# Residual and read-back products at the end of an expert pass placed elsewhere in TensorE's order, one tile's second result added by VectorE

## The reference

```python
combine = jnp.sum(jax.nn.one_hot(e_idx, N_EXPERTS, dtype=F32) * weights[..., None], axis=1)
a = jnp.einsum('td,edf->tef', x, w_gate)
b = jnp.einsum('td,edf->tef', x, w_up)
hid = jax.nn.silu(a) * b * combine[:, :, None].astype(x.dtype)
y = jnp.einsum('tef,efd->td', hid, w_down)
...
x = x + g2 * hierarchical_moe(h, ...)
```

## Time and profile before

| what | value |
|---|---|
| runs | 787.0, 788.08, 793.8 us, median 788.08 |
| span of the profiled execution | 789.8 us, its only recorded time |
| TensorE busy | 663.3 us, 84% |
| VectorE busy | 295.1 us, 37% |
| ScalarE, GpSimd busy | 132.0 us, 121.6 us |
| DMA over the span | 369 GB/s on average, 291.11 MB |
| share of the chain that ended last | PE 64%, DMA 27%, DVE 4% |

### The profile page before, as it was taken

The page is one execution under the profiler, slowest core; times in us unless marked ns, Lnnn a source line. Parts: engine busy times, 40 slices in busy tenths (PEclk is TensorE's granted clock), DMA queues, the critical chain, the costliest instruction groups (busy, mean ns, idle before and its releaser), DMA issues.

```text
span 789.8 us, 12765 instructions
## 1 busy us (share of the span) xinstructions
PE 663.3 (84%) x4709; PEld 361.2 (46%) x4709; DVE 295.1 (37%) x723; ACT 132.0 (17%) x328; POOL 121.6 (15%) x194
## 2 busy tenths in 40 slices
PE   3899999999998999999546668998999997564576
PEld 3443443446886855554213223648655553221232
DVE  2305518664217434444211131555444443112123
ACT  3111134553045100000000000653000000000000
POOL 1000000001000223333221010010234334111010
PEclk9999999999998899999866788998999999677679
DMA  9999859868189389999999999997599999999995
GB/s 334 426 429 428 335 224 395 353 284 356 56 357 395 121 354 418 420 418 417 421 423 421 423 420 350 426 424 316 184 420 416 419 420 421 423 421 419 421 403 232
DMA packets 39577, 291.11 MB, mean 369 GB/s; under 512 B 7466, under 2 KB 8898, under 8 KB 20448
## 3 DMA queue, kind: packets, MB, share of 16 engines
q1 hardware_dynamic: 30112, 272.46, 83.5%
q0 software_dynamic: 7600, 12.81, 4.7%
q10 hardware_dynamic: 1808, 5.06, 1.6%
HBM read 284.68 MB, written 17.56 MB: 383 GB/s over the span
## 4 chain that ended last, share of the span: by engine, by line
PE 64%; DMA 27%; DVE 4%; SPq 2%; issue 1%; ACT 1%; DVEq 0%; ACTq 0%
PE bank L1725 17%; DMA adaw<-in_moe_w_in 9%; PE bank L1430 8%; DMA ring<-in_moe_w_in 8%; PE bank L1762 7%; DMA adas<-in_moe_w_in 7%; PE bank L1355 4%; PE bank L1529 4%; DMA ring<-in_ada_w 3%; PE bank L1684 2%; PE bank L1537 2%; PE bank L1468 2%; PE bank L1489 2%; PE bank L1644 2%; PE bank L1592 1%; PE bank L1500 1%
## 5 line engine op out<-in xcount | busy, mean ns | idle before, releaser
L1725 PE MATMUL bank<-ring,qkv 128*32 128x256 f32 (+1 forms) x1344 | 140.7, 447 | 46.6 <-DMA ring<-in_moe_w_in 33.6
L1725 PEld LDWEIGHTS bank<-ring,qkv 128*32 128x32 f32 (+1 forms) x1344 | 78.2, 139 | 93.4 <-issue 66.8
L1201 DVE COPY qkv<-bank 128x512 f32<-128x512 f32 x44 | 30.5, 692 | 205.9 <-PE bank L1684 205.9
L603 POOL DMA_INDIRECT results<-adaw,scur x46 | 47.3, 1029 | 265.0 <-DVE adaw L1224 226.3
L868 ACT ACTIVATE qkv<-bank 128x128 f32<-128x128 f32 x48 | 13.3, 278 | 419.2 <-PE bank L1725 419.2
L1762 PE MATMUL bank<-ring,qkv 128*32 128x512 f32 (+1 forms) x368 | 65.7, 601 | 0.0
L1430 PE MATMUL bank<-ring,hT 128*128 128x512 f32 x144 | 63.8, 597 | 1.3 <-DVE hT L948 1.3
L1725 PE MATMUL bank<-seventh,qkv 128*64 128x256 f32 (+1 forms) x224 | 34.8, 478 | 16.4 <-DMA ring<-in_moe_w_in 16.4
L593 POOL DMA_INDIRECT adaw<-rows,gcur x40 | 41.7, 1042 | 33.0 <-POOL gcur L590 27.7
L1725 PE MATMUL bank<-adaw,qkv 128*64 128x256 f32 (+1 forms) x256 | 35.8, 442 | 10.0 <-DMA adas<-in_moe_w_in 10.0
L1430 PEld LDWEIGHTS bank<-ring,hT 128*128 128x128 f32 x144 | 26.7, 190 | 37.0 <-issue 35.8
(11 more groups left out here) (265 smaller groups left out, 856.2 us busy)
## 6 DMA issues: line engine op xcount, KB each, us to landing
ring<-in_moe_w_in SPq DMA_DIRECT2D x37, 2048.0 KB, 20.7
ring<-in_moe_w_out SPq DMA_DIRECT2D x44, 1024.0 KB, 24.1
ring<-in_ada_w SPq DMA_DIRECT2D x14, 2048.0 KB, 14.8
adaw<-in_ada_w SPq DMA_DIRECT2D x10, 2048.0 KB, 16.0
adaw<-in_moe_w_in SPq DMA_DIRECT2D x8, 2048.0 KB, 23.6
seventh<-in_moe_w_in SPq DMA_DIRECT2D x8, 1792.0 KB, 26.2
xT<-in_moe_w_in SPq DMA_DIRECT2D x8, 1536.0 KB, 19.1
hT<-in_moe_w_out SPq DMA_DIRECT2D x10, 1024.0 KB, 26.2
```

The lines of the kernel that those rows point to most:

```text
L603: pool.indirect_dma_start(res, bass.IndirectOffsetOnAxis(ap=scur[:, p, :], axis=0), yout[:, p], None, bounds_check=res_limit, oob_is_err=F ...
L1201: V.tensor_copy(xgT[:, p], bank[2][:, :]).then_inc(xgT_ready, 1)
L1725: last = T.matmul(bank[p][64 * a + m * h:64 * a + m * (h + 1), 0:2 * P], xk[:, k % 4, k // 4, m * h:m * (h + 1)], gate_up_of(b, k)[:, :, a ...
```

## The change

It moves three things and replaces one.

1. On TensorE `residual` of the first tile stands ahead of the second-last `step`, that of the third tile behind it (with a wait for the last row transpose's copy), that of the second tile behind `down(NS - 2)` and a wait for VectorE's result of tile NS - 2. All three are ahead of the last `gate_up`.
2. The first tile's second-result product stands ahead of the one-hot products, the second tile's behind them.
3. The third tile (token tile 0) has no second-result product; VectorE adds that result to xtok with one 128x1024 add, after it has added the first. `sum_mm` counts in another order, and VectorE adds the first results in the order tile 1, tile 0, tile 2.
4. The read-backs come in the order second, first for the first two tiles, first, second for the third.

```diff
                 sp.wait_ge(results_in, l + 1)
-                for t in TILES_BACK:
-                    for k in range(2):
+                for n, t in enumerate(TILES_BACK):
+                    for k in ((1, 0), (1, 0), (0, 1))[n]:
...
+            def first_result(l, t, n):
                 dve.wait_ge(s_xin[t][0], l * 16 + 16)
-                dve.wait_ge(sum_mm, l * TT + n + 1)
+                dve.wait_ge(sum_mm, l * TT + n)
...
+            def summed(l, n):
+                t = TILES_BACK[n]
+                if n == 0:
+                    first_result(l, t, 1).then_inc(x_sum, 1)
+                    order(first_result(l, TILES_BACK[2], 2))
+                elif n == 1:
+                    first_result(l, t, 3).then_inc(x_sum, 1)
+                else:
+                    dve.wait_ge(s_xin[t][1], l * 16 + 16)
+                    V.tensor_tensor(xtok[:, t, :], xtok[:, t, :], parts[t][:, 1, :], ALU.add).then_inc(x_sum, 1)
...
-                for s in range(1, NS - 1):
+                for s in range(1, NS - 2):
                     step(s)
...
                 residual(TILES_BACK[0])
+                step(NS - 2)
+                pe.wait_ge(xgT_ready, l * NS + NS)
+                residual(TILES_BACK[2])
                 down(NS - 2, (NS - 2) % 2)
+                pe.wait_ge(y_ready, l * NS + NS - 1)
+                residual(TILES_BACK[1])
                 gate_up(NS - 1, (NS - 1) % 2)
                 hidden_T(NS - 1, (NS - 1) % 2)
-                pe.wait_ge(y_ready, l * NS + NS - 1)
-                residual(TILES_BACK[1])
-                residual(TILES_BACK[2])
                 down(NS - 1, (NS - 1) % 2)
...
+                second_result(TILES_BACK[0], False)
+                pe.wait_ge(y_ready, l * NS + NS)
+                last_tile(TILES_BACK[0], True).then_inc(sum_mm, 1)
+                last_tile(TILES_BACK[1], False)
+                last_tile(TILES_BACK[2], True).then_inc(sum_mm, 1)
+                second_result(TILES_BACK[1], True).then_inc(sum_mm, 1)
```

More of the change, by code:

```diff
@@ L1297, in scale_tile @@
                 V.tensor_scalar(part, part, ss[:, 12 + t:13 + t], None, ALU.mult).then_inc(band_ready, 1)
-            def summed(l, n):
-                t = TILES_BACK[n]
+            def first_result(l, t, n):
                 dve.wait_ge(s_xin[t][0], l * 16 + 16)
-                dve.wait_ge(sum_mm, l * TT + n + 1)
+                dve.wait_ge(sum_mm, l * TT + n)
                 for a, b in enumerate(SUM_BANKS[t]):
@@ L1307, in summed @@
                         order(last)
-                last.then_inc(x_sum, 1)
+                return last
+            def summed(l, n):
[8 more added lines that the diff above has]
+                    V.tensor_tensor(xtok[:, t, :], xtok[:, t, :], parts[t][:, 1, :], ALU.add).then_inc(x_sum, 1)
             scales(1, 1, 8)
@@ L1815, in _, with second_result, last_tile @@
                     residual(TILES_BACK[2])
-                pe.wait_ge(y_ready, l * NS + NS)
-                for t in TILES_BACK:
+                def second_result(t, stop):
+                    pe.wait_ge(s_xin[t][1], l * 16 + 16)
+                    for a, b in enumerate(SUM_BANKS[t]):
+                        last = T.matmul(bank[b][:, :], ident, parts[t][:, 1, a * 512:(a + 1) * 512], start=False, stop=stop,
+                                        skip_group_check=True)
+                    return last
+                def last_tile(t, stop):
                     for a, b in enumerate(SUM_BANKS[t]):
                         half = slice(64 * a, 64 * a + 64)
[L1820 to L1825, removed]
-                                        skip_group_check=True)
-                    last.then_inc(sum_mm, 1)
+                        last = T.matmul(bank[b][:, :], dg[half, t], yout[half, (NS - 1) % NBUF], start=False, stop=stop,
+                                        skip_group_check=True)
+                    return last
+                second_result(TILES_BACK[0], False)
[4 more added lines that the diff above has]
+                second_result(TILES_BACK[1], True).then_inc(sum_mm, 1)
                 if l == 0:
```

## The result

| | kernel before | changed kernel |
|---|---|---|
| runs and median | 20 runs, 790.64 us | 20 runs, 787.03 us |
| ratio to before | | 0.9943, 95% interval 0.9923 to 0.9963 |
| profiled span | 789.8 us | 785.6 us |

By the ratio the change gains 0.57%, 4.5 us (2.9 to 6.1). The three runs that stood ahead of the prediction had a median of 788.08; with twenty the kernel before is at 790.64. The medians are 3.6 us apart, which lies inside the same interval. A fp32 product stands in all these traces as two records, so four records are the two products of a tile.

What follows compares the result with a forecast made beforehand. The prediction took TensorE's chain of products, behind each pass's last gate product, to bound the pass ends. Gains of 4.3 and 4.7 us minus 2.2 for the clock gave 6.8: 788.08 - 6.8 = 781.3 us, range 778.0 to 786.0.

Steps and rivals of the forecast that it cites:

- the price of the clock: TensorE's new pauses in both passes may drop the clock to 1.2 GHz: 0 to 4.5 us, taken as 2.2.
- step 1: Two residual tiles leave TensorE's path ahead of the last down product, which starts 3.0 us sooner in pass 1.
- Step 2 and 3: Closing read-back products and VectorE's reordered sums in pass 1: last sum ends at 496.7 us, before at 499.91.
- Step 4: From pass 1's last sum to the next stage's windows 2.23 us: windows at 498.95 instead of 503.23, 4.3 us gained.
- The second pass: Pass 2 moves with pass 1's gain; at its end the last add comes at 782.05 instead of 786.77, 4.7 us.
- rival B: Both new TensorE pauses cost their full clock price: 788.08 - 4.5 = 783.6 us; chance 0.22 together with E.
- Rival A: The clock costs nothing in either pass: 788.08 - 9.0 = 779.1 us; chance 0.22.
- Rival C: Read-backs land later, so VectorE's hold is 2 us longer in each pass, on top of the clock: 785.3; chance 0.10.
- D: Fifth read-back lands so late, 6 us in each pass, that the kernel gets slower: 791 us; chance 0.04.
- E: New wait for VectorE's result delays the last gate product, so residuals stay on the path: about 784; 0.22 with B.

Runs made afterwards that it cites:

- the two agreeing profiles: Second and third profile of the unchanged kernel before; the three stretches sum to 307.4 us in each, against 310.7 in its first profile.
- the sums alone: Changed kernel with the residual products where they were before; only the new read-back order, second-result products and VectorE sums remain; ratio 0.9961 (0.9926 to 0.9997), 3.1 us.
- the second set: Second timing of the kernel before with only the residual products moved: 12 runs, ratio 1.0004 (0.9975 to 1.0033); the first timing gave 1.0028 in 10 runs.

## Why the prediction was right or wrong

The forecast was 781.3 with a range of 778.0 to 786.0; measured are 787.03, outside. In the difference it was 6.8 us against 4.5 (2.9 to 6.1). Of the 5.7 us between 781.3 and 787.03, 2.6 are the base: I subtracted from a median of three runs that lay that much below the one of twenty. The rest is the difference, 6.8 forecast and 3.6 between the medians. The mechanism held: the residuals left the path, the sums got shorter, and TensorE lost its clock in the new waits. The step that failed is the price of the clock: the prediction took 2.2 us for both passes, and found were 3.4 (part of it VectorE's hold), and 1.0 more between the passes, a stretch that it took as fixed. The next largest is step 1, sized on one profile. Term by term, in us, measured as means of three profiles of each kernel:

| term | forecast | measured |
|---|---|---|
| down product sooner, pass 1 | 3.0 | 2.2 |
| down product sooner, pass 2 | 2.7 | 2.7 |
| sums, pass 1, at 2.4 GHz | 1.3 | 2.0 |
| sums, pass 2, at 2.4 GHz | 2.0 | 1.4 |
| clock, and hold beyond it, both passes | -2.2 | -3.4 |
| between the passes (M) | 0 | -1.0 |
| behind the last add | 0 | -0.2 |
| sum | 6.8 | 3.7 |

- **Step 1, the residuals off the path.** The mechanism holds: the down product starts 7.8 and 8.0 us behind the gate product's start. Against the first profile these are 3.2 and 2.7 us (forecast 3.0 and 2.7), but the other two profiles of the kernel before have 9.5 and 9.4 in pass 1, so against them it is 1.6 there. The term was mis-sized because one profile's clock was taken as the kernel's. That the down weight "does not bind by 0.3 us" in pass 1 was wrong too: with the gate product at full clock TensorE waits 2.4 us for it. I had seen this for pass 2 alone.
- **Step 2 and 3, the sums.** 2.0 us in pass 1 and 1.4 in pass 2 with the clock at 2.4 GHz (forecast 1.3 and 2.0). The forecast had 7.7 us from the down product's start to the end of the last product; at 2.4 GHz it is 8.4. The last add took 1.22 us, forecast 1.2. VectorE's hold for the fifth read-back, for which the forecast has 2.1 us in pass 1 (490.0 to 492.1), came there in one of three profiles of the changed kernel (2.03 us) and in two of the filled versions (1.91 and 1.73), and never in pass 2. It follows the late issue of the read-backs.
- **Step 4.** From the last add to the windows 2.3 us, forecast 2.2.
- **The second pass.** The prediction lets it start sooner by all that pass 1 won. M is not constant: 252.7 to 256.5 us over all profiles, with the clock's sags in it, and 1.0 us longer in the changed kernel on the mean (1.6 against the two agreeing profiles). Whether the change causes that is open.
- **The clock.** This is the step that failed in size. I took half of 4.5 us. In pass 2 the fall at the down product costs 1.65 us (12.87 from its start to the last add, against 11.22 in three of the runs that fill the wait and in the one with the sums alone), in all three profiles of the change, so its full price, which I had at 1.7. In pass 1 it is 1.65 at the down product, or 2.1 with the hold and slow windows (20.37 and 20.86 from the down product's start to the pooling, against 18.7), one of the two in each execution of the change. Of the 2.1 the hold is 1.25 (the last add ends 13.07 us behind the down product's start instead of 11.82) and the windows' clock 0.9, where the prediction had 2.8. The wait for the down weight in pass 1, at which the clock fell in two of the three, stands in the prediction as not binding. So rival B, both pauses at full price, 788.08 - 4.5, had the right difference by luck: it has 1.7 + 2.8 where 1.65 and 1.65 to 2.1 were found, no loss in M, and a larger gain ahead of them.
- Rival A fell with the clock. Rival C, a hold longer by 2 us in each pass than counted, did not come, nor did D: the latest hold seen ends at 494.2 us, and D needs 496.3. E did not come: the last gate product starts when its weights land, 0.70 us after the residual product in front of it.

That the clock falls during the wait for the down weight, and that work in this wait prevents it, is shown for pass 2 by three edits (a residual product of the first tile, one of the second, filler products). There the down product takes 3.2 to 3.6 us in all eight profiles that leave the wait empty and 1.92 or 1.93 in all seven that have work in it. In pass 1 it is slow in three of the eight and in none of the seven, which fits, but behind five empty waits of 2.2 to 2.4 us it is at full clock. Nor did filling the wait shorten pass 1: S1p is 28.1 to 28.6 in the four filled profiles with the order of sums of the change, which has 28.2 to 28.6.

Not settled is why the residual moves alone give nothing in time when the means of three profiles say 1.6 us. Against the two agreeing profiles they say 0.5 us, which the second set admits (0.25% faster, 2.0 us, to 0.33% slower) and the first just excludes. Nor is it settled why the clock survives some waits in pass 1. The late read-backs go with the hold and the slow windows, as told above; they also go with a down product at full clock in five of the six unfilled profiles that have them, which no run explains.

## What to carry to other kernels

Where TensorE waits for weights at the end of a chain, find the last weight that it will wait for and put work that has no deadline into that wait. Ahead of an earlier wait the same products look free, but they leave a pause in front of the critical product. Here that cost 1.65 us of clock at the end of pass 2. At the end of pass 1 filling the pause made the stretch no shorter: of four filled profiles two had VectorE held by a read-back, one a later weight, and one a gate product at half rate. A gate product at half rate cost little as long as a later weight was the bound. And take two or three profiles of the kernel before: of a difference of 4 us between single profiles, 3.3 us were the clock of one execution.

## What was not expected of the hardware

- The same program, with the same sequence of products, has its clock fall at different places from one execution to the next: last gate product 6.56 or 4.98 us, first window records 1.20 or 2.18 us, M 255.7 or 253.8 us.
- From GpSimd's last scatter in pass 1 to the read-backs that wait for it, it takes 6.5 to 6.7 us in seven profiles and 7.7 to 8.0 in twelve, and nothing between.
- TensorE stopped once for 1.36 us between two records of one row of one-hot products, which wait for nothing; in no other profile was it there at this place. Its cause is open.
